# Convolution and scan of a three-block kernel: memory steps behind the weight items, two sums ahead of a tile's taps, chunk loads ahead of small vectors

## The chip, the cores and the metric

The kernel runs as one program on one core of a Trainium2 chip. The metric is the device time of an execution in microseconds; runs of the kernel before took 3612.26, 3619.60 and 3623.09 us (median 3619.6). One execution more was profiled: it took 3616.24 us. PE is TensorE, DVE VectorE, ACT ScalarE, POOL GpSimd; SP only issues transfers.

## The reference, cut to what matters

Three transformer-like blocks follow one another over 1024 positions of width 1024. The change lies in the first, with one piece of work of the second beside it:

```
proj = h @ w_in                                   # h (1024, 1024)
z, xbc, dt_f, dt_b, q, k, v, g = split(proj)
xbc = silu(centred_dwconv(xbc, conv_w, conv_b))   # 5 taps in time, by channel
xs, Bm, Cm = split(xbc)                           # 1024 + 256 + 256 channels
y = bidirectional_ssd(xs, softplus(dt + bias), A, Bm, Cm, D)   # chunks of 128 positions
lam = exp(sum(lq1*lk1)) - exp(sum(lq2*lk2)) + lam_init
```

Inside `bidirectional_ssd`, each direction sums `dt * A` over the time steps of a chunk (`a_cs`), takes exponentials of the sums and of their differences to the chunk's end, and carries a state from chunk to chunk. The second block attends to a memory of 256 rows; its keys and values, `mem_2 @ w_mem_kv_2`, depend on no activation and are computed beside the convolution of block one ("memory" below).

## The kernel before

Every engine has its own instruction list, written out by hand, and runs it in order; engines wait for each other through counting semaphores. There is no planner: the order in the functions is the order on the engine.

**Convolution (`sp_conv`, `pe_conv`, `act_conv`, `dve_conv`, `pool_conv`).** The projection comes in items of 128 channels. For an item SP loads a 512 KB weight slice, ACT makes its high part (`act_item`, L490), DVE its low part (`dve_item`, L497), and PE does 48 products of 128 x 512 (L508: three combinations of high and low, 8 slices of the inner dimension, 2 halves) into one of two PSUM pairs. Item 0 gives the time steps `dt`, items 1 to 12 the twelve channel tiles of `xbc`, items from 13 on queries and keys, which PE works off in quarters during the scan. In round r PE transposes the finished tile of two rounds before (the "turn"; tiles 10 and 11, at r = 4 and 5, have none) and does item r + 1. ACT in round r copies the turned tile out (L606, L610), applies silu to the tile before (L617), copies item r + 1 out of PSUM (`raw`, L622, which raises `conv_raw`), and makes the high part of item r + 3. DVE in round r waits for that copy (L683), does the five taps (L693 to L697), the low part of item r + 3, and then a piece of the time steps' chain (r = 2 to 5), memory's low part (r = 6, `dve_memory`, L1927), the sums (r = 8, L709 to L712) or `dt_end` (r = 9).

**Memory.** `pe_memory` has three steps, at r = 4, 5 and 6, ahead of the round's item: 8 transposes, 8 transposes, 64 products of 128 x 256 (L184) into banks 6 and 7. ACT copies each step's result as the last thing of the round (`act_memory`, L1918, L1920, L1921); step 1 waits for step 0's copy, step 2 for step 1's. The turn at r = 7 uses the same banks and waits for both of the last step's results:

```
if n == 3:
    pe.wait_ge(S["mem_out"], 3)
    pe.wait_ge(S["mem_lo"], 1)
```

**Sums.** At r = 8, behind item 9, PE forms the sums of `dtA` (6 small products, banks 6 and 7, `cum_mm`). DVE copies them to `cum` and subtracts (`cum_sub`); ACT exponentiates (`carry`, L636, first). The turn at r = 9 uses bank 7 again and waits for `carry` (`steps` at 1, in the list of PE).

**Scan.** `conv_over` makes each engine wait until the last turned tile has been stored to DRAM. Then SP issues, in this order: the gate vector `gssm` and four lambda vectors (each broadcast to 128 partitions), the first chunk of `xs` (512 KB), the spills of two query halves (`qk_out`, two transfers each), the second chunk. POOL scales the first chunk (L1041), PE makes the first state from it (L897, after three quarters of queries and keys), DVE copies the state. Eight rounds go backward in time, eight forward. `lambda_dots` (L1087 to L1093) comes first in DVE's list for the scan; its result is read by ACT after the backward rounds (L1001), `gssm` by DVE in the forward rounds (L1175). SP's transfers go through `Transfers.start` (L124): there are 8 semaphores in turn, and each issue waits until the transfer eight places before it has landed.

Of the kernel before, what the change touches and what calls it, by code (L numbers as in the profile page):

```python
# [8 lines left out]
S = 1024  # L9
# [154 lines left out]
def rows(vector, n=P):  # L164
    return vector.partition_broadcast(n)
# [371 lines left out]
def pe_conv(K):  # L537
    pe, S, m = K.pe, K.S, K.p2

    def item(n):  # L540
        pe.wait_ge(S["it_lo"], n + 1)
        for q in range(4):
            last = item_quarter(K, n, K.pair[n % 2], q)
        last.then_inc(S["it_mm"], 1)

    pe.wait_ge(S["nat_act"], NAT_N)
    item(0)
    for r in range(14):
        turn = r - 2
        if r == 13:  # L550
            pe_quarters(K, QK_FIRST)
        if turn >= 0 and CONV_TILES[turn] < 10:
            done = K.BT[:, CONV_TILES[turn] - 8] if CONV_TILES[turn] >= 8 else m.acc[turn % 3]
            n = turn if turn < 2 else turn - 2
            if n == 1:
                pe.wait_ge(S["dt_v"], 1)
            elif n == 5:
                pe.wait_ge(S["steps"], 1)
            if n >= 2:
                pe.wait_ge(S["conv_out"], n - 1)  # L560
            if n == 3:
                pe.wait_ge(S["mem_out"], 3)
                pe.wait_ge(S["mem_lo"], 1)
            pe.wait_ge(S["conv_silu"], turn + 1)
            transposed(pe, K.pair[2 + n % 2], [done[:, s * P:(s + 1) * P] for s in range(ST)], K.eye).then_inc(S["conv_turned"], 1)
        if 4 <= r < 7:
            pe_memory(K, r - 4)
        if r < 12:
            if r >= 1:
                pe.wait_ge(S["conv_raw"], r - 1) if r >= 2 else pe.wait_ge(S["dt_copied"], 1)  # L570
            item(r + 1)
        if r == 1:
            for st in range(ST):
                last = pe.transpose(K.bank[6][:, st * 32:(st + 1) * 32], m.dtT[0:32, st * P:(st + 1) * P], K.eye[0:32, 0:32])
            last.then_inc(S["dt_turned"], 1)
        if r == 8:
            pe.wait_ge(S["dtA"], 1)
            pe.wait_ge(*K.loads["upper"])
            pe.wait_ge(*K.loads["lower"])
            pe.wait_ge(S["conv_out"], 4)  # L580
            products(pe, K.bank[6][:, 0:128], [(K.upper, K.dtA[:, :, 0:16])])
            products(pe, K.bank[6][:, 128:256], [(K.lower, K.dtA[:, :, 16:32])])
            products(pe, K.bank[7][:, 0:256], [(K.ones, K.dtA)]).then_inc(S["cum_mm"], 1)
# [57 lines left out]
def dve_conv(K):  # L641
    v, S, vs, m = K.v, K.S, K.vs, K.p2

    def then(instruction):
        vs.mark(instruction)
        v.wait_ge(vs.sem, vs.n)

    v.wait_ge(S["nat_mm"], 5 * ST)
    for n in range(2):
        dve_item(K, n)  # L650
    norm_over(K, v)
    for raw in m.raw:
        vs.mark(v.memset(raw[:, 0:2], 0.0))
        vs.mark(v.memset(raw[:, 2 + S_LEN:], 0.0))
    v.wait_ge(vs.sem, vs.n)
    V, u, z, z2, dt = K.spare, K.dtA, K.cum, K.to_end, K.dt
    dve_item(K, 2)

    def time_steps():
        v.wait_ge(S["dt_u"], 1)  # L660
        then(v.tensor_scalar(z, u, 2.0, None, ALU.add))
        then(v.reciprocal(z, z))
        then(v.tensor_tensor(z, z, u, ALU.mult))
        then(v.tensor_tensor(z2, z, z, ALU.mult))
        then(v.tensor_scalar(dt, z2, 1.0 / 19, 1.0 / 17, ALU.mult, ALU.add))
        for n in range(15, 0, -2):
            then(v.tensor_tensor(dt, dt, z2, ALU.mult))
            then(v.tensor_scalar(dt, dt, 1.0 / n, None, ALU.add))
            if n in (13, 7, 3):
                yield  # L670
        then(v.tensor_tensor(dt, dt, z, ALU.mult))
        then(v.tensor_scalar(V, V, 0.0, None, ALU.max))
        then(v.scalar_tensor_tensor(dt, dt, 2.0, V, ALU.mult, ALU.add))
        v.wait_ge(S["A_exp"], 1)
        then(v.tensor_scalar(K.A32, K.A32, -1.0, None, ALU.mult))
        v.tensor_tensor(K.dtA, dt, over(K.A32, 1, ST), ALU.mult).then_inc(S["dtA"], 1)
        yield

    steps = time_steps()
    v.wait_ge(*K.loads["conv_w"])  # L680
    for r in range(12):
        tile = CONV_TILES[r]
        v.wait_ge(S["conv_raw"], r + 1)  # L683
        if r >= 3:
            old = CONV_TILES[r - 3]
            if old < 10:
                v.wait_ge(S["conv_turned"], (r - 3 if r - 3 < 2 else r - 5) + 1)
            v.wait_ge(S["conv_silu"], r - 2)
        raw, acc = m.raw[r % 2], m.acc[r % 3]
        for j in range(TAPS):  # L690
            tap = K.convw[:, tile, j:j + 1]
            if j == 0:
                then(v.tensor_scalar(acc, raw[:, 0:S_LEN], tap, None, ALU.mult))  # L693
            elif j < TAPS - 1:
                then(v.scalar_tensor_tensor(acc, raw[:, j:j + S_LEN], tap, acc, ALU.mult, ALU.add))
            else:
                v.scalar_tensor_tensor(acc, raw[:, j:j + S_LEN], tap, acc, ALU.mult, ALU.add).then_inc(S["conv_tap"], 1)  # L697
        dve_item(K, r + 3)
        if r == 1:
            v.wait_ge(S["dt_turned"], 1)  # L700
            v.wait_ge(*K.loads["dt_bias0"])
            v.wait_ge(*K.loads["dt_bias1"])
            v.tensor_tensor(V, K.bank[6][:, 0:256].rearrange("p (s n) -> p s n", s=ST), over(K.bias32, 1, ST), ALU.add).then_inc(S["dt_v"], 1)
        if 2 <= r < 6:
            next(steps)
        if r == 6:
            dve_memory(K)
        if r == 8:
            v.wait_ge(S["cum_mm"], 1)  # L709
            sums = K.bank[6][:, 0:256].rearrange("p (d s h) -> p s d h", d=2, s=ST)  # L710
            then(v.tensor_copy(K.cum.rearrange("p s (d h) -> p s d h", d=2), sums))
            v.tensor_tensor(K.to_end, K.bank[7][:, 0:256].rearrange("p (s n) -> p s n", s=ST), K.cum, ALU.subtract).then_inc(S["cum_sub"], 1)  # L712
        if r == 9:
            v.wait_ge(S["steps"], 2)
            v.tensor_tensor(K.dt_end, dt, K.to_end, ALU.mult).then_inc(S["dt_end"], 1)
    dve_quarters(K, QK_FIRST)
# [97 lines left out]
def sp_scan(K):  # L814

    sp, S, L, m = K.sp, K.S, K.loads, K.p3
    conv_over(K, sp)
    L.start(sp, "gssm", m.gssm, rows(K.dr["ssm_norm_g"][0]))
    for i, n in enumerate(("lambda_q1", "lambda_k1", "lambda_q2", "lambda_k2")):
        L.start(sp, n, K.p4.lq[:, i], rows(K.dr[n][0]))  # L820

    def chunk(r):
        if 2 <= r < ST + 2:
            sp.wait_ge(S["sc_xfree"], r - 1)
        elif r >= ST + 2:
            sp.wait_ge(S["sc_y"], 2 * (r - 2 - ST) + 2)
        if r < 2 * ST:
            L.start(sp, ("xs", r), m.xs[r % 2], K.xs_dram[CHUNKS[r]])

    def gate(c):  # L830
        if c:
            sp.wait_ge(S["sc_ms"], c)
        L.start(sp, ("zg", c), m.zg, K.nat_dram["z"][c])

    def back(c):

        if c >= ST:
            return
        if c >= 2:
            sp.wait_ge(S["sc_yadd"], 2 * (c - 1) + 1)  # L840
        for done in (0, 1):
            sp.wait_ge(*K.stores[("yb", done)])
        L.start(sp, ("yb", c), m.yb if c else m.y[0], K.yb_dram[c])

    def parts(x):

        cols = slice(x % 2 * 512, (x % 2 + 1) * 512)
        sp.wait_ge(S["qk_lo"], x + 1)
        for part in range(2):
            L.start(sp, ("qk_out", x, part), K.qk_dram[x // 2, part][:, cols], m.qk[x % 3][part].bitcast(F32))  # L850

    def quarters(ks):
        for k in ks:
            if k % 4 == 0 and k:
                sp_item(K, QK_ITEM + k // 4 + 2)
            if k % 2:
                parts(k // 2)

    chunk(0)
    quarters(QK_FIRST)  # L860
    chunk(1)
    for r in range(2 * ST):
        if r == ST:
            back(0)
        if r >= ST:
            gate(r - ST)
            back(r - ST + 1)
        for place in QK_PLAN[r]:
            quarters(place)
        chunk(r + 2)  # L870
# [233 lines left out]
def dve_scan(K):  # L1104
# [72 lines left out]
                vs.mark(last)  # L1177
        last.then_inc(S["sc_yn"], 1)

    lambda_dots(K)  # L1180
    v.wait_ge(*K.loads["eye"])
    vs.mark(v.tensor_tensor(K.below, K.lower, K.eye, ALU.subtract))
    vs.mark(v.tensor_tensor(K.above, K.upper, K.eye, ALU.subtract))
# [3 lines left out]
    for b in range(ST):  # L1187
# [12 lines left out]
        if b < ST - 1:  # L1200
            new_state(("bnew", b), b == 0)
        dve_quarters(K, QK_PLAN[b][2])
    lambda_sum(K)
    masked(0)
    both(0, 0)
# [2514 lines left out]
```

## Time and profile before

| | |
|---|---|
| three runs | 3612.26, 3619.60, 3623.09 us |
| profiled execution: time, span | 3616.24 us, 3614.4 us |
| PE busy in the span | 3141.3 us (87%) |
| DVE, ACT, POOL busy | 2060.6 (57%), 1197.4 (33%), 436.6 (12%) us |
| mean granted clock of PE | 0.94 |
| convolution (item 0 to last chunk stored) | about 316 to 534 us |
| backward half, forward half of the scan | about 534 to 676, to 915 us |

Times inside the profile count from the first instruction. A group's name is "output <- inputs" by the program's tile names; `banks` is PSUM. The bracket at the end of a timeline row is how long the engine was idle before the instruction and what ended it. Matmuls overlap, so their single durations add up to more than the time they take: the distance from start to start is the time. The granted clock is a share of the full 2.4 GHz.

### The profile page before, as it was taken

The numbers are of one execution on the slowest core, as the hardware profiler recorded it, in microseconds if no ns is written. First come the engines' busy times: TensorE is split into PE (matmuls) and PEld (weight loads), VectorE is DVE, ScalarE is ACT, GpSimd is POOL, SyncE is SP. The second block draws the span as 40 slices with busy tenths as digits, with TensorE's granted clock in tenths as the row PEclk, the third lists the DMA queues.
The fourth block names the chain that finished last, engine by engine and source line by source line (L and its number), as shares of the span: only waits on it lengthen the run. The fifth ranks groups of instructions, "written<-read, shape, count | busy, mean of one in ns | idle before, by whom it ended". The sixth has DMA issues, their size and how long they took to land. (4 is left out here: it accounts for less than half of the span.)

```text
span 3614.4 us, 37560 instructions
## 1 busy us (share of the span) xinstructions
PE 3141.3 (87%) x14208; PEld 2393.5 (66%) x14208; DVE 2060.6 (57%) x3113; ACT 1197.4 (33%) x2280; POOL 436.6 (12%) x407
## 2 busy tenths in 40 slices
PE   6999889886788879899997762989976989999999
PEld 5787667664677768677885552444554468888887
DVE  5112544487688835839886876549865334444444
ACT  2211231586566632234225651000264011112111
POOL 2000002344011100222340031010000000000000
PEclk9999999997899999999998986999988999999999
DMA  6323125433633334341462410411011011111111
GB/s 215 134 72 101 42 83 189 140 119 103 165 94 94 88 143 149 99 101 53 129 201 85 129 59 31 161 69 56 14 35 62 0 47 47 47 47 47 47 58 59
DMA packets 189934, 326.63 MB, mean 90 GB/s; under 512 B 16242, under 2 KB 110610, under 8 KB 189754
## 3 DMA queue, kind: packets, MB, share of 16 engines
q1 hardware_dynamic: 168602, 250.29, 22.7%
q0 software_dynamic: 21152, 73.94, 5.7%
q8 instruction: 114, 1.87, 0.2%
q14 instruction: 66, 0.54, 0.1%
HBM read 233.71 MB, written 89.16 MB: 89 GB/s over the span
## 5 line engine op out<-in xcount | busy, mean ns | idle before, releaser
L215 PE MATMUL banks<-b3h4a_hi,b3mlpw_part 128*128 128x512 f32 x1024 | 319.8, 391 | 6.8 <-DVE b3mlpw_part L3277 6.8
L215 PE MATMUL banks<-b3mlpw_part,b3mlp_acthi 128*128 128x512 f32 x1024 | 315.2, 389 | 0.0
L215 PE MATMUL banks<-b1ln_w,b_hThi 128*128 128x512 f32 x768 | 239.5, 393 | 0.0
L215 PEld LDWEIGHTS banks<-b3h4a_hi,b3mlpw_part 128*128 128x128 f32 x1024 | 193.7, 189 | 47.5 <-issue 7.1
L215 PEld LDWEIGHTS banks<-b3mlpw_part,b3mlp_acthi 128*128 128x128 f32 x1024 | 192.2, 188 | 39.9
L3324 DVE TENSOR_TENSOR b3out_x<-b3out_x,banks 128x1024 f32<-128x1024 f32 x128 | 154.8, 1219 | 111.6 <-PE banks L215 111.6
L215 PE MATMUL banks<-b3out_lo,b3mlpw_part 128*128 128x512 f32 x512 | 200.4, 391 | 0.0
L215 PE MATMUL banks<-b3mlpw_part,b3mlp_actlo 128*128 128x512 f32 x512 | 199.2, 389 | 0.0
L508 PE MATMUL banks<-b_hThi,b1item_hi 128*128 128x512 f32 x464 | 196.2, 423 | 3.4 <-DVE b1item_lo L497 3.1
L3294 ACT ACTIVATE b3mlp_relu<-banks 128x1024 f32<-128x1024 f32 x32 | 32.9, 1029 | 499.5 <-PE banks L215 499.5
L508 PE MATMUL banks<-b_hThi,b1item_lo 128*128 128x512 f32 x464 | 183.4, 395 | 0.0
L508 PE MATMUL banks<-b_hTlo,b1item_hi 128*128 128x512 f32 x464 | 183.4, 395 | 0.0
L2131 PE MATMUL banks<-b2h_hi,b2h_whi 128*128 128x512 f32 (+1 forms) x448 | 177.9, 397 | 5.9 <-issue 5.9
L1370 ACT ACTIVATE b1att_map<-b1att_map,fixed_stat 128x1024 f32<-128x1024 f32 x128 | 147.0, 1149 | 104.5 <-DVE fixed_stat L1419 104.1
L2320 DVE MAX8 b2late_top<-b2late_sel 128x8 f32<-128x384 f32 (+5 forms) x192 | 170.9, 890 | 16.8 <-DMA dv_spill<-b2ring_row 13.1
L3313 DVE TENSOR_TENSOR b3mlp_relu<-b3mlp_relu 128x1024 f32<-128x1024 f32 x32 | 39.2, 1225 | 243.5 <-ACT b3mlp_relu L3294 243.5
L2131 PE MATMUL banks<-b2h_lo,b2h_whi 128*128 128x512 f32 (+1 forms) x448 | 176.6, 394 | 0.0
L2131 PE MATMUL banks<-b2h_hi,b2h_wlo 128*128 128x512 f32 (+1 forms) x448 | 176.3, 393 | 0.0
L2322 DVE MATCH_REPLACE8 b2late_sel<-b2late_top,b2late_sel 128x384 f32<-128x384 f32 (+5 forms) x192 | 168.2, 876 | 0.0
L215 PEld LDWEIGHTS banks<-b1ln_w,b_hThi 128*128 128x128 f32 x768 | 144.6, 190 | 32.8 <-ACT b1ln_out L377 1.7
L1419 DVE CUSTOM_DVE_ANT_0 b1att_map<-banks,b1att_dist 128x1024 f32<-128x1024 f32 x128 | 151.6, 1222 | 0.6
L215 PE MATMUL banks<-b1ln_w,b_hTlo 128*128 128x512 f32 x384 | 150.3, 391 | 0.0
(417 smaller groups left out, 6716.8 us busy)
## 6 DMA issues: line engine op xcount, KB each, us to landing
qk_spill<-b1scan_qk SPq DMA_DIRECT2D x64, 256.0 KB, 2.8
b1att_k<-qk_spill SPq DMA_DIRECT2D x64, 256.0 KB, 8.2
b1out_ws<-in_w_out SPq DMA_DIRECT2D x16, 1024.0 KB, 5.0
b3mlpw_stage<-in_w_mlp_up SPq DMA_DIRECT2D x16, 1024.0 KB, 5.3
b3mlpw_stage<-in_w_mlp_down SPq DMA_DIRECT2D x16, 1024.0 KB, 4.9
b2h_stage<-in_w_in SPq DMA_DIRECT2D x30, 512.0 KB, 4.1
b1item_stage<-in_w_in SPq DMA_DIRECT2D x29, 512.0 KB, 4.9
b1ln_stage<-in_w_in SPq DMA_DIRECT2D x12, 1024.0 KB, 6.8
```

The costliest lines, as they stand in the source:

```text
L215: last = pe.matmul(out, x, y, start=i == 0, stop=i == n - 1)
L508: last = K.pe.matmul(pair[:, ss], a, b, start=q % 2 == 0 and i == 0, stop=q % 2 == 1 and i == 11)
L1370: a.activation(mp, mp, ACT.Exp, bias=s[:, i:i + 1], scale=-1.0, accum_out=s[:, 2 + i:3 + i]).then_inc(S["att_exp"], 1)
L1419: v.tensor_tensor_reduce(mp, K.pair[1 + i], m.dist[:, x0:x0 + S_LEN], -1.0, 3e38, ALU.add, ALU.min, s[:, i:i + 1]).then_inc(S["att_shift"], 1)
L2131: last = pe.matmul(K.bank[x % 2][0:w], a[:, k, 0:w], b[:, k, ss], start=part == 0 and i == 0, stop=part == 1 and i == 11)
L2320: vs.mark(v.max(top, view))
L2322: vs.mark(v.match_replace(view, top, view, TAKEN))
L3294: a.activation(m.tmp[i % 3], pair, ACT.Relu).then_inc(S["ml_relu"], 1)
L3313: v.tensor_tensor(tmp, tmp, tmp, ALU.mult).then_inc(S["ml_sq"], 1)
L3324: v.tensor_tensor(K.m4.x3[:, st], K.m4.x3[:, st], pair, ALU.add).then_inc(S["ml_acc"], 1)
```

## The change

Three edits of order, with no arithmetic added or left out. On PE, at r = 4, 5, 6, the memory step stands behind the round's item. On DVE, at r = 8, the copy of the sums and the subtraction stand ahead of the wait for the round's raw tile. In the scan SP issues the first two chunks first, then the lambda vectors, the first spills, and then the gate vector; DVE does the lambda dot products behind the first backward round.

```diff
@@ pe_conv @@
-        if 4 <= r < 7:
-            pe_memory(K, r - 4)
         if r < 12:
             if r >= 1:
                 pe.wait_ge(S["conv_raw"], r - 1) if r >= 2 else pe.wait_ge(S["dt_copied"], 1)
             item(r + 1)
+        if 4 <= r < 7:
+            pe_memory(K, r - 4)
@@ dve_conv @@
     for r in range(12):
         tile = CONV_TILES[r]
+        if r == 8:
+            v.wait_ge(S["cum_mm"], 1)
+            sums = K.bank[6][:, 0:256].rearrange("p (d s h) -> p s d h", d=2, s=ST)
+            then(v.tensor_copy(K.cum.rearrange("p s (d h) -> p s d h", d=2), sums))
+            v.tensor_tensor(K.to_end, K.bank[7][:, 0:256].rearrange("p (s n) -> p s n", s=ST), K.cum, ALU.subtract).then_inc(S["cum_sub"], 1)
         v.wait_ge(S["conv_raw"], r + 1)
...
         if r == 6:
             dve_memory(K)
-        if r == 8:
-            v.wait_ge(S["cum_mm"], 1)
-            sums = K.bank[6][:, 0:256].rearrange("p (d s h) -> p s d h", d=2, s=ST)
-            then(v.tensor_copy(K.cum.rearrange("p s (d h) -> p s d h", d=2), sums))
-            v.tensor_tensor(K.to_end, K.bank[7][:, 0:256].rearrange("p (s n) -> p s n", s=ST), K.cum, ALU.subtract).then_inc(S["cum_sub"], 1)
@@ sp_scan @@
     conv_over(K, sp)
-    L.start(sp, "gssm", m.gssm, rows(K.dr["ssm_norm_g"][0]))
-    for i, n in enumerate(("lambda_q1", "lambda_k1", "lambda_q2", "lambda_k2")):
-        L.start(sp, n, K.p4.lq[:, i], rows(K.dr[n][0]))
...
     chunk(0)
+    chunk(1)
+    for i, n in enumerate(("lambda_q1", "lambda_k1", "lambda_q2", "lambda_k2")):
+        L.start(sp, n, K.p4.lq[:, i], rows(K.dr[n][0]))
     quarters(QK_FIRST)
-    chunk(1)
+    L.start(sp, "gssm", m.gssm, rows(K.dr["ssm_norm_g"][0]))
@@ dve_scan @@
-    lambda_dots(K)
     v.wait_ge(*K.loads["eye"])
...
         dve_quarters(K, QK_PLAN[b][2])
+        if b == 0:
+            lambda_dots(K)
```

## Rows read from the trace of the kernel before

**Rows 1.** The page, busy time by engine: us, share of the span, instructions.
```profile
PE 3141.3 (87%) x14208; PEld 2393.5 (66%) x14208; DVE 2060.6 (57%) x3113; ACT 1197.4 (33%) x2280; POOL 436.6 (12%) x407
```

**Rows 2.** Waits of PE, 374 to 476.2 us: total us, times, longest.
```profile
PE banks L206 <- DVE b1conv_mk L1927: 9.1, 1, 9.1
PE banks L206 <- ACT b1ssm_carry L636: 8.7, 1, 8.7
PE banks L206 <- ACT b1conv_memT L1918: 3.0, 1, 3.0
PE banks L184 <- ACT b1conv_memT L1918: 2.2, 1, 2.2
```

**Rows 3.** Timeline of PE: start us, us, engine, line, operation, [idle before <- releaser].
```profile
404.36 5.38 PE L184 MATMUL banks<-b1conv_memT,b1conv_wkv 128*128 128x256 f32 x16 [2.19 <-ACT b1conv_memT L1918]
...
409.57 3.62 PE L184 MATMUL banks<-b1conv_wkv,b1conv_memT 128*128 128x256 f32 x16
...
440.15 1.94 PE L206 MATMUL banks<-fixed_eye,b1conv_acc 128*128 128x128 f32 x8 [9.12 <-DVE b1conv_mk L1927]
...
454.47 1.03 PE L206 MATMUL banks<-fixed_eye,b1conv_acc 128*128 128x128 f32 x8
...
466.69 0.60 PE L184 MATMUL banks<-b1ssm_dtA,fixed_ones 128*128 128x256 f32 x2
...
475.94 1.97 PE L206 MATMUL banks<-fixed_eye,b1conv_acc 128*128 128x128 f32 x8 [8.65 <-ACT b1ssm_carry L636]
...
489.48 1.04 PE L206 MATMUL banks<-fixed_eye,b1conv_acc 128*128 128x128 f32 x8
...
501.25 1.04 PE L206 MATMUL banks<-fixed_eye,b1conv_acc 128*128 128x128 f32 x8
```

**Rows 4.** Busy time in four stretches; after POOL the granted clock, DMA share, GB/s.
```profile
386.30:389.30 3.00, 0.03 (x2) 0.02 (x1) 1.80 (x2) 2.88 (x3) 0.00 (x0) 1.00 0.00 0
454.50:466.30 11.80, 11.80 (x58) 9.90 (x57) 7.03 (x6) 4.05 (x4) 0.89 (x1) 1.00 0.31 90
467.30:476.00 8.70, 0.06 (x1) 0.06 (x1) 7.79 (x8) 2.90 (x5) 0.00 (x0) 0.61 0.03 3
555.00:675.00 120.00, 119.07 (x479) 89.30 (x477) 55.65 (x53) 19.08 (x27) 26.58 (x18) 1.00 0.55 180
```

**Rows 5.** Timeline of ScalarE, round 6 and round 8.
```profile
432.93 0.59 ACT L1920 ACTIVATE b1conv_mk<-banks 128x512 fp32r<-128x512 f32 x1
...
468.44 1.28 ACT L636 ACT_TABLE_LOAD   x1
475.51 0.38 ACT L636 ACTIVATE b1ssm_carry<-banks 128x256 f32<-128x256 f32 x1 [5.79 <-DVE b1ssm_to_end L712]
```

**Rows 6.** Timeline of VectorE, round 6 and round 8.
```profile
439.21 0.68 DVE L1927 TENSOR_TENSOR b1conv_mk<-banks,b1conv_mk 128x512 fp32r<-128x512 f32 x1
...
467.51 0.75 DVE L693 TENSOR_SCALAR b1conv_acc<-b1conv_raw,b1ssm_convw 128x1024 f32<-128x1024 f32 x1 [4.61 <-ACT b1conv_raw L622]
...
474.60 0.42 DVE L711 COPY b1ssm_cum<-banks 128x256 f32<-128x256 f32 x1
475.05 0.42 DVE L712 TENSOR_TENSOR b1ssm_to_end<-banks,b1ssm_cum 128x256 f32<-128x256 f32 x1
```

**Rows 7.** Timeline of all engines at the scan's front (SPq: transfers issued by SP).
```profile
533.93 0.34 SPq L128 DMA_DIRECT2D b1scan_gssm<-in_ssm_norm_g  x1
...
536.22 0.43 SPq L128 DMA_DIRECT2D b1scan_xs<-x_spill  x1
...
541.84 0.23 DVE L1093 CUSTOM_DVE_ANT_0 b1ssm_spare<-b1ssm_spare 128x64 f32<-128x64 f32 x1 [13.42 <-DMA b1ssm_spare<-in_lambda_k]
...
543.04 1.90 POOL L1041 TENSOR_TENSOR b1scan_scaled<-b1scan_xs,b1ssm_dt_end 128x1024 f32<-128x1024 f32 x1 [12.37 <-DMA b1scan_xs<-x_spill]
...
545.08 1.19 PE L897 MATMUL banks<-b1scan_scaled,b1ssm_B 128*128 128x512 f32 x1 [10.45 <-POOL b1scan_scaled L1041]
```

**Rows 8.** The chunk tile `xs` of the scan: its 16 loads, issue to landing.
```profile
DMA to landing us min/median/max: 3.7/5.2/5.7
```

## The prediction

> **What bounds the kernel now.** I read the page first: one core, and of its span of 3614.4 us TensorE (PE) is busy 87% [rows 1]. The share says little about a change that touches only some 300 us of the first block, so I went to the waits of PE in the stretch from the first memory transposes to the second half of the convolution. In these 102 us PE stands still four times, 23.0 us in all: twice for ScalarE's copy of the transposed memory (2.97 and 2.19 us), once for VectorE's low part of the memory keys (9.12), once for ScalarE's exponential `carry` (8.65) [rows 2]. The timeline of PE then shows what a wait costs beyond itself. A regular tile (8 transposes and a weight item of 48 products) takes 489.48 to 501.25 = 11.77 us; the tile after the 9.12 us wait takes 440.15 to 454.47 = 14.32, the one after the 8.65 us wait 475.94 to 489.48 = 13.54, and the first 16 memory products 5.38 us where the next 16 take 3.62 [rows 3]. Over the 8.65 us wait the granted clock averages 0.61, so it went from 2.4 to 1.2 GHz in it; over the wait of 2.97 us it stayed at 1.00 [rows 4]. Outside these waits PE is dense here: in the undisturbed tile from 454.5 to 466.3 us PE is busy 11.80 of 11.80, VectorE, with its taps and an item's low part, 7.03 [rows 4]. So in this stretch each microsecond that PE no longer waits should end the stretch earlier by one, and its lateness is handed on: from 555 to 675 us PE is busy 119.07 of 120 at clock 1.00 [rows 4], and the stages after that start from what PE has finished.
>
> **Part 1: memory's steps behind the items.** PE is in order. At r = 4, 5, 6 it now does item r + 1 first and then the memory step. Nothing the item needs is later than before: its low part was made two rounds earlier, its PSUM pair was emptied a round and a half earlier. The copy of the first transposes by ScalarE now has an item of 11 us beside it, as has that of the second. Both waits (2.97 + 2.19 = 5.2 us) go. Split the 11.77 us of a tile into 0.8 for transposes and 11.0 for the item, and count from the start of round 4: item 5 ends at 11.0, memory 0 at 11.8, item 6 at 22.8, memory 1 at 23.6, the turn at 24.4, item 7 at 35.4. The 64 memory products follow: their four groups of 16 take 3.5 us each (the next group starts a little before the 3.62 are over; the first took 5.38 for the slow clock, 1.76 more), so until 49.3. What is late next is the turn at r = 7, which still needs both memory results. Before, the high copy by ScalarE came at 432.93 although the products had long ended, as it sat behind the copy of item 7's result, and VectorE's subtraction at 439.21, behind five taps and an item [rows 5, 6]. Now item 7 ends 13.9 us ahead of the products: ScalarE has copied it about 1 us later, VectorE has done taps and low part 7 us after that, at 43.6, and both stand ready 5.7 us early. The new wait is 0.59 + 0.68 and two hand-overs, 1.5 us. Queued behind it on PE is item 8, and ScalarE's round 7. The 9.12 becomes 1.5, and at 1.5 us I expect the clock to hold, as it did over 2.97: of 14.32 us the tile gives back 14.32 - 11.77 = 2.55.
> Sum of part 1: 2.97 + 2.19 + 9.12 + 1.76 + 2.55 - 1.5 = 17.1 us. If the clock falls all the same it is 14.5, the lower end; 18.6 (no wait left) is the upper.
>
> **Part 2: the sums ahead of the taps at r = 8.** VectorE's copy and subtraction (0.42 each, at 474.60 and 475.05) move ahead of the wait for the tile's raw copy. PE's last sum ends at 466.69 + 0.60 = 467.29 [rows 3]; VectorE is idle then (4.61 us until its taps at 467.51 [rows 6]), so both are done by about 468.25. ScalarE has its raw copy and item copy first, then a table load from 468.44 to 469.72, which before stood ahead of its wait [rows 5]; the exponential of 0.38 now follows at once and ends at 470.1. PE's turn starts at 470.15 in place of 475.94: 5.8 us. The table load is what is late next. The price is that this tile's taps start at about 468.3 in place of 467.51, 0.8 us; PE needs their result only a full tile (11.77 us) later, against 7.0 us of work: nothing. VectorE parked ahead of the taps would cost something only if the sums came after the raw copy by more than that slack; before, they came within 0.2 us of it.
> The clock: PE then rests 467.29 to 470.15, 2.9 us. The rows show both answers for about this length: 1.00 throughout in one rest of 2.97 us [rows 4], and slow products at 404.36 after a rest of 2.19 behind light transposes [rows 3]. The sums are short too, so I leave the lost 13.54 - 11.77 = 1.8 us where it is. Part 2 gives 5.8, with ends at 5.0 (the taps' delay passed on once) and 7.6.
>
> **Part 3: the scan's front.** SP issued the gate vector at 533.93, four lambda rows, and the first chunk at 536.22; GpSimd began on it at 543.04, 12.37 us idle, and PE on the first state at 545.08 [rows 7]. Now the chunk is issued first: 2.3 us by the issue times alone, if it then takes as long as before. Before, it needed 543.04 - 536.22 = 6.8 us to be used, the longest way among the chunk loads, which land in 3.7 to 5.7 us, median 5.2 [rows 8]; ahead of it were 512 KB of the vector and the lambda rows, the last of which reached VectorE only at 541.84 [rows 7]. Issued first at 533.93 it is usable at 533.93 + 3.8 = 537.7 at best and 539.7 at worst, a gain of 5.3 to 3.4. The second chunk directly behind it carries another 512 KB, and so I take a way of 4.6 us, between the shortest and the median, which is a gain of 4.5. The low end is 2.3, the high end 5.3.
> The Trainium skill (DMA: Bandwidth & Descriptors, Queues, rings and completion order) says that each DMA engine takes descriptors in the order of its ring. By that the second chunk can't hold up the first, and part 3 would be 5.3 and the whole sum 28.2; the rows don't show two chunks back to back.
> VectorE's wait for the lambda rows (13.42 us, until 541.84) goes from the front; it held back nothing that PE waited for, and the dot products (0.23 us and a little more, twice) now lie beside a busy PE. ScalarE wants them only behind the backward half, and the gate vector is read in the forward half. On SP the lambda issues and the four spills now stand ahead of the vector; each issue waits for the one eight places earlier, so the next item load goes out about when it did, and PE asks for it five quarters of an item later, at 11.0 / 4 = 2.8 us each: nothing. If it were late by the longest landing of a load of its size here, 5.7 us [rows 8], so much would be lost again.
>
> **The sum.** 17.1 + 5.8 + 4.5 = 27.4 us. The profiled execution took 3616.24 us, 1.8 more than its span: 3588.8 from its own time. It lies 3.4 under the median of the three runs, 3619.6, and 2.1 under their mean, 3618.3. I take the mean as the base: 3590.9, told as 3591. The parts' ends give 14.5 + 5.0 + 2.3 = 21.8 to 18.6 + 7.6 + 5.3 = 31.5 us.
>
> **Rivals.**
> *A, the forecast*, 3591, 82%.
> *B, the memory's subtraction stays late.* If VectorE were still in its taps when the high copy comes, the wait at r = 7 would be about 9 us again and with it the slow clock: 27.4 - 7.6 - 2.55 = 17.2, so 3601. For it: exactly this order made the 9.12. Against: taps begin with item 7's copy, and copy, taps and low part are 8.2 us against 13.9 of memory products. 6%.
> *C, the gain is handed on only in part.* A load or a later stage takes over (the item load behind the lambda rows, the chunk loads, the attention's front) and gives back half: 3605. Against: item loads are issued two rounds ahead, 23 us against landings of 5.7, and PE is 99% busy behind. 5%.
> *D, it does nothing that shows*: the stretch is bound by another engine, 3615 to 3620. Against: VectorE and ScalarE themselves wait on PE here. 4%.
> *E, slower: the clock pays it back.* Without these rests PE runs dense from 374 to 675. If it were then held at 1.2 GHz, each microsecond of work would take two: from 27 us of such work on it decides, and 40 us of the backward scan held down would end at 3631. For it: nothing in the rows but that the clock is granted and taken. Against: 120 us at 99% busy kept 1.00 [rows 4]. 3%. The Trainium skill (TensorE: Matmul & The Clock Gate, Part 1) knows such a limit only once three cores of a die run dense matmuls; here one does.
>
> **The numbers.** A measurement of this kernel tells about 0.3%, 11 us, from no change: 3629 and 3607 are the bounds around the mean. A, B and nearly all of C are faster: 0.92; D and the rest of C the same: 0.05; E slower: 0.03. The range reaches from A's upper end with the spread of the runs, 3583, to beyond B, 3603.
>
> **What would show it.** PE's waits for `memT` gone; the turn at r = 7 waiting 1.5 us for `mk`, the one at r = 9 about 2.9 for `carry`; the 64 memory products in 13.9 us; the last convolution tile 23 us earlier, GpSimd's first scaled chunk 3.8 to 5.8 us after SP's first issue, PE's wait for it 6 in place of 10.45 us. Wrong if the wait for `mk` stays above 5 us, if tiles between grow beyond 11.8, if GpSimd's first operation comes later than 6 us after the issue, or if the 27 us are there at 550 and gone at 900.

## The result, and the profile after

The changed kernel takes 3592.02 us (median of 6 runs, 3587.31 to 3594.58) against 3621.24 us for the kernel before on the same chip (6 runs, 3612.26 to 3624.18): ratio 0.9921, 95% interval 0.9908 to 0.9934, so 0.8% or 29 us faster. Run a second time beside 21 runs of the kernel before (median 3618.35) it took 3592.25, ratio 0.9932 (0.9919 to 0.9944), 26 us. The forecast was 3591, with 27.4 us gained. The profiled execution took 3593.28 us, its span is 3591.5, 22.9 us under that of before.

The page after, span and busy time (as [rows 1]):

```profile
span 3591.5 us, 37561 instructions
...
PE 3146.4 (88%) x14208; PEld 2400.0 (67%) x14208; DVE 2061.1 (57%) x3113; ACT 1198.3 (33%) x2280; POOL 435.1 (12%) x407
```

The waits of TensorE (PE) from 374 to 460 us, as in [rows 2] (total us, times, longest). Of the four waits the two for `memT` are gone, and 9.1 and 8.7 us have become 1.6 and 2.9:

```profile
PE banks L206 <- ACT b1ssm_carry L636: 2.9, 1, 2.9
PE banks L206 <- DVE b1conv_mk L1928: 1.6, 1, 1.6
```

PE's timeline, as in [rows 3]. All four groups of memory products take 3.62 us now. The tile behind the wait for the keys takes 423.91 to 435.74 = 11.83 us, a regular one; the tile behind the wait for `carry` 451.43 to 464.91 = 13.48 (before 13.54):

```profile
408.32 3.62 PE L184 MATMUL banks<-b1conv_memT,b1conv_wkv 128*128 128x256 f32 x16
411.77 3.62 PE L184 MATMUL banks<-b1conv_wkv,b1conv_memT 128*128 128x256 f32 x16
...
423.91 1.06 PE L206 MATMUL banks<-fixed_eye,b1conv_acc 128*128 128x128 f32 x8 [1.61 <-DVE b1conv_mk L1928]
...
435.74 1.04 PE L206 MATMUL banks<-fixed_eye,b1conv_acc 128*128 128x128 f32 x8
...
447.95 0.60 PE L184 MATMUL banks<-b1ssm_dtA,fixed_ones 128*128 128x256 f32 x2
451.43 1.73 PE L206 MATMUL banks<-fixed_eye,b1conv_acc 128*128 128x128 f32 x8 [2.88 <-ACT b1ssm_carry L636]
...
464.91 1.04 PE L206 MATMUL banks<-fixed_eye,b1conv_acc 128*128 128x128 f32 x8
```

What released the two waits, ScalarE (ACT) first, VectorE (DVE) second; they answer to [rows 5, 6]. The low part of the keys now comes right behind the high part; the sums come ahead of the taps; the exponential comes right behind its table load:

```profile
422.33 0.60 ACT L1921 ACTIVATE b1conv_mk<-banks 128x512 fp32r<-128x512 f32 x1 [11.84 <-PE banks L184]
...
449.70 1.28 ACT L636 ACT_TABLE_LOAD   x1
450.99 0.38 ACT L636 ACTIVATE b1ssm_carry<-banks 128x256 f32<-128x256 f32 x1
```

```profile
422.97 0.69 DVE L1928 TENSOR_TENSOR b1conv_mk<-banks,b1conv_mk 128x512 fp32r<-128x512 f32 x1 [6.21 <-ACT b1conv_mk L1921]
...
448.59 0.42 DVE L686 COPY b1ssm_cum<-banks 128x256 f32<-128x256 f32 x1 [4.41 <-PE banks L184]
449.05 0.42 DVE L687 TENSOR_TENSOR b1ssm_to_end<-banks,b1ssm_cum 128x256 f32<-128x256 f32 x1
449.39 0.74 DVE L698 TENSOR_SCALAR b1conv_acc<-b1conv_raw,b1ssm_convw 128x1024 f32<-128x1024 f32 x1
```

Busy time in four stretches, as in [rows 4] (behind POOL the granted clock): the rest ahead of the keys, the tile behind it, the rest ahead of `carry`, and what followed it. The clock stays at 1.00 in both rests, holds after the first and falls to 1.2 GHz after the second:

```profile
421.80:424.00 2.20, 0.59 (x4) 0.21 (x3) 0.69 (x1) 1.09 (x2) 0.00 (x0) 1.00 0.00 0
424.00:436.00 12.00, 12.00 (x59) 10.04 (x60) 0.00 (x0) 2.12 (x3) 0.89 (x1) 1.00 0.15 45
448.50:451.40 2.90, 0.05 (x1) 0.00 (x0) 2.74 (x4) 2.87 (x5) 0.00 (x0) 1.00 0.00 0
451.40:455.00 3.60, 3.57 (x13) 3.18 (x14) 3.49 (x4) 2.37 (x4) 0.49 (x1) 0.54 0.02 5
```

The scan's front, as in [rows 7], and the landings of the chunk loads, as in [rows 8]. GpSimd begins 513.02 - 509.37 = 3.65 us after the first issue, in the kernel before 543.04 - 533.93 = 9.11; PE waits 5.01 in place of 10.45 us. The pair shown here is the widest one: over the profiles of this study this way takes 8.46 to 9.11 us in the three kernels with the old order of SP and 3.65 to 4.04 us in the eight profiles with the new one, so part 3 is worth 4.4 to 5.5 us there. The rows:

```profile
509.37 0.81 SPq L128 DMA_DIRECT2D b1scan_xs<-x_spill  x2
...
510.23 0.42 SPq L128 DMA_DIRECT2D b1ssm_spare<-in_lambda_q  x1
...
513.02 1.90 POOL L1041 TENSOR_TENSOR b1scan_scaled<-b1scan_xs,b1ssm_dt_end 128x1024 f32<-128x1024 f32 x1 [6.91 <-DMA b1scan_xs<-x_spill]
514.69 0.33 SPq L128 DMA_DIRECT2D b1scan_gssm<-in_ssm_norm_g  x1
...
515.06 3.75 PE L897 MATMUL banks<-b1scan_scaled,b1ssm_B 128*128 128x512 f32 x4 [5.01 <-POOL b1scan_scaled L1041]
...
525.17 0.22 DVE L1093 CUSTOM_DVE_ANT_0 b1ssm_spare<-b1ssm_spare 128x64 f32<-128x64 f32 x1
```

```profile
DMA to landing us min/median/max: 3.5/4.4/6.4
```

The start times of the same work in both profiles show where the time came from and where some of it went again:

| starts at, us | before | after | earlier by |
|---|---|---|---|
| first item's products | 315.6 | 314.3 | 1.3 |
| last of the sums | 466.7 | 448.0 | 18.7 |
| turn at r = 9 | 475.9 | 451.4 | 24.5 |
| first state | 545.1 | 515.1 | 30.0 |
| first, last product of `R` in the forward half | 681.4, 884.4 | 650.9, 857.0 | 30.5, 27.4 |
| first attention scores | 909.4 | 882.1 | 27.3 |
| last relu of the third block's MLP | 3566.4 | 3543.5 | 22.9 |

The 1.3 us at the top lie ahead of any change. From there to the turn at r = 9 the gain is 23.2 us, from there to the first state another 5.5, 28.7 in all.

### The profile page after: what moved, and what is told of

It reads as the page before. It is cut to its first block and busy times, and to the rows that moved or that the text cites. A ratio compares the mean times of both kernels' runs of the same rounds, so it can differ in the third digit from the quotient of the medians.

```text
span 3591.5 us, 37561 instructions
## 1 busy us (share of the span) xinstructions
PE 3146.4 (88%) x14208; PEld 2400.0 (67%) x14208; DVE 2061.1 (57%) x3113; ACT 1198.3 (33%) x2280; POOL 435.1 (12%) x407
```

## The experiments

**Each part alone, and the whole once more.** Three kernels hold one of the three edits each, as the diff of the change shows it; the fourth is the changed kernel unaltered. All four are compared with the same 21 runs of the kernel before.

> Part 1 alone (memory's steps behind the items), all else as before. My theory: 17.1 us shorter than the kernel before, the wait for memT gone, the wait for the memory keys 1.5 us, the wait for carry still 8.7 and the wait for the first scaled chunk still 10.5. Rival (the three parts are not additive, the wait for carry only shows since others were removed or grows): under 12 us. Rival (the subtraction stays behind the taps): 10 us, with a wait of about 9 for the keys.

Measured: 3603.59 us against 3618.35, ratio 0.9961 (0.9949 to 0.9974), 14.8 us by the medians, 9 to 18 by the interval. In its trace the sums start at 448.0 and the first item at 314.3, to the tenth as in the changed kernel, so the stretch gained the same 17.4 us. PE's waits there, with those for `carry` and for the chunk still in place:

```profile
PE banks L897 <- POOL b1scan_scaled L1041: 9.8, 1, 9.8
PE banks L206 <- ACT b1ssm_carry L636: 8.7, 1, 8.7
PE banks L206 <- DVE b1conv_mk L1927: 1.6, 1, 1.6
```

> Part 2 alone (the sums ahead of the taps at r = 8). My theory: 5.8 us shorter; the wait for carry 2.9 in place of 8.65 us, the tile behind it still slow (13 to 13.5 us). If the clock holds over 2.9 us: 7.6. Rival (the later taps are handed on to PE): 5.0 or less, and the next turns come late. Rival (nothing, the stretch is bound elsewhere): 0.

Measured: 3613.11 against 3618.35, ratio 0.9986 (0.9977 to 0.9995), 5.2 us. The wait for `carry` is 2.9 us, the four others as before. From the sums to the first state it gained 7.2 - 0.4 = 6.8 us by start times, of which 0.7 belong to a shorter wait for the chunk (9.8 against 10.5).

> Part 3 alone (first two chunks, then lambda, spills, gate vector; lambda dots behind the first backward round). My theory: 4.5 us shorter, up to 5.5, with PE's wait for the first scaled chunk 5 to 6 in place of 10.45 us. Rival (the later order of SP's transfers costs the forward half or the attention's front what the front gains, which would explain that in the changed kernel 30.5 us at the first forward chunk are 27.3 at the first attention scores): 0 to 2 us shorter in total, and the forward half some 3 us longer than in the kernel before.

Measured: 3614.52 against 3618.35, ratio 0.9993 (0.9984 to 1.0002). The 3.8 us by the medians are not clear of nothing in the times alone; the trace has PE's wait at 5.1 in place of 10.45 us and the first state 7.2 - 1.9 = 5.3 us earlier than the sums. Its forward half took 673.7 to 880.0 = 206.3 us, 3.3 more than in the kernel before, as the rival has it. But the kernels with part 1 and part 2 alone, whose scan is that of the kernel before, took 208.0 and 207.8 us there, so this is no cost of part 3.

> The changed kernel once more, nothing altered. Theory (what is lost behind the front, 30.5 us at the first forward chunk to 22.9 at the end of the span, is mostly chance of single executions, the clock's turns above all): the forward half of the scan takes 204 to 207 us in this profile, not the same as in the first one, and the ratio is again 0.992. Rival (a cost of the change itself): again 207 us for the forward half and the same losses behind it.

Measured: 3592.25 us, ratio 0.9932 (0.9919 to 0.9944). The forward half took 208.1 us (652.0 to 860.1) where the first profile of the same kernel took 206.1: its length is not fixed by the code. Over the fourteen profiles of this study it took 202.9 to 203.0 us in six (the kernel before and five altered ones), 206.0 to 206.3 in four, and 207.8 to 208.1 in four. The 3 us that the pair of profiles loses there go with no edit; that they are the chance of single executions fits the repeated kernel, and fits that the profiled execution of before (3616.24) is faster than its kernel's medians (3617 to 3621), but with one profile of before it is not shown. The stretch behind it, from the last product of `R` to the last relu of the third block, varies as well: 2682.0 us before, 2686.5 in the first profile of the changed kernel, 2684.0 in the repeated one; of the fourteen profiles the kernel before has the shortest. So of the 4.5 us that the pair loses there, 2.5 go with no edit. The three parts' gains, 14.8 + 5.2 + 3.8 = 23.8 us, stand beside 26.1 for the whole against the same runs; the difference is within the intervals.

**Memory's last step alone put back.** In the changed kernel the 64 products stand ahead of item 7 again:

```diff
+        if r == 6:
+            pe_memory(K, 2)
         if r < 12:
...
-        if 4 <= r < 7:
+        if 4 <= r < 6:
             pe_memory(K, r - 4)
```

> The changed kernel with one thing undone: at r = 6 the 64 memory products stand ahead of item 7 again, while the two transposing steps stay behind their items. My theory (VectorE's subtraction gets behind the taps by this order alone, and a wait this long brings the slow clock): PE's wait for the keys 9.1 in place of 1.6 us, the tile behind it 14.3 in place of 11.8, so 10 us slower than the changed kernel and 16 us faster than the kernel before. Rival (the waits for memT, 5.2 us, carried most of part 1): 5 us slower than the changed kernel or less.

Measured: 3601.97 us, ratio 0.9952 (0.9940 to 0.9964); 9.7 us slower than the changed kernel's 3592.25, or 7 to 11 us by the ratios (0.9932 and 0.9921), as the two were measured on different chips. PE's timeline has the wait and the slow tile back, 430.72 to 444.66 = 13.94 us:

```profile
396.60 3.69 PE L184 MATMUL banks<-b1conv_memT,b1conv_wkv 128*128 128x256 f32 x16 [1.32 <-ACT b1conv_memT L1921]
...
430.72 1.94 PE L206 MATMUL banks<-fixed_eye,b1conv_acc 128*128 128x128 f32 x8 [9.15 <-DVE b1conv_mk L1930]
...
444.66 1.04 PE L206 MATMUL banks<-fixed_eye,b1conv_acc 128*128 128x128 f32 x8
```

From the turn at r = 2 to the last of the sums the trace has 456.87 - 347.07 = 109.8 us where the changed kernel has 447.95 - 349.35 = 98.6: 11.2 us longer (counted from there, as item 0 ran partly at the low clock in the changed kernel's profile, 0.72 over 314 to 320 us, and not in this one), of which 1.32 are a wait for `memT` that this order brings back. So the order of this one step is worth more than half of the 17.4 us of part 1, and the rest is in the main the two short waits for `memT` and the slow products behind the second. The rival, 5 us or less, is out by the trace.

**What held the first chunk back.** Three orders of SP at the scan's front, one profile each, all else as changed: the gate vector first; the four lambda vectors first; the second chunk behind the spills.

```diff
 # gate vector first
+    L.start(sp, "gssm", m.gssm, rows(K.dr["ssm_norm_g"][0]))
     chunk(0)
...
 # lambda vectors first
+    for i, n in enumerate(("lambda_q1", "lambda_k1", "lambda_q2", "lambda_k2")):
+        L.start(sp, n, K.p4.lq[:, i], rows(K.dr[n][0]))
     chunk(0)
...
 # second chunk late
     chunk(0)
-    chunk(1)
...
     quarters(QK_FIRST)
+    chunk(1)
```

> The changed kernel with the gate vector (512 KB broadcast) issued ahead of the first chunk. Theory 1 (bytes ahead in the queue hold the chunk back): GpSimd begins 5 to 6 us after SP's first issue where the changed kernel has 3.65 us, and PE waits 6.5 to 7 in place of 5.0. Theory 2 (the four small lambda broadcasts did it): GpSimd begins 4.1 us after the first issue, 0.4 later by the issue alone, PE waits 5.4.

> The changed kernel with the four lambda vectors (32 KB each, in pieces of 256 bytes) issued ahead of the first chunk. Theory 1 (bytes count): GpSimd begins 5.7 us after SP's first issue, 1.9 us for the four issues and 0.1 for 128 KB more. Theory 2 (the small pieces are slow, few bytes moved from 537 to 539 us in the kernel before): 7 us or more after the first issue, and PE waits 8.3 us or more.

> The changed kernel with the second chunk's load behind the first spills again. By the prediction's choice (the second chunk behind the first holds it up by some 0.9 us) GpSimd would begin 2.8 us after SP's first issue in place of 3.65; by the ring rule there is no difference, 3.65, as the first chunk is served first.

First issue and GpSimd's start in the timelines, gate vector first, then lambda first, then with the second chunk late:

```profile
509.79 0.34 SPq L128 DMA_DIRECT2D b1scan_gssm<-in_ssm_norm_g  x1
...
510.18 0.90 SPq L128 DMA_DIRECT2D b1scan_xs<-x_spill  x2
...
515.72 1.90 POOL L1041 TENSOR_TENSOR b1scan_scaled<-b1scan_xs,b1ssm_dt_end 128x1024 f32<-128x1024 f32 x1 [9.17 <-DMA b1scan_xs<-x_spill]
```

```profile
509.59 0.34 SPq L128 DMA_DIRECT2D b1ssm_spare<-in_lambda_q  x1
...
511.40 0.90 SPq L128 DMA_DIRECT2D b1scan_xs<-x_spill  x2
...
518.19 1.90 POOL L1041 TENSOR_TENSOR b1scan_scaled<-b1scan_xs,b1ssm_dt_end 128x1024 f32<-128x1024 f32 x1 [11.85 <-DMA b1scan_xs<-x_spill]
```

```profile
509.27 0.34 SPq L128 DMA_DIRECT2D b1scan_xs<-x_spill  x1
...
512.78 1.90 POOL L1041 TENSOR_TENSOR b1scan_scaled<-b1scan_xs,b1ssm_dt_end 128x1024 f32<-128x1024 f32 x1 [6.76 <-DMA b1ssm_spare<-in_lambda_k]
```

In the last of these rows the profile names a lambda row as what ended the wait; GpSimd's list waits there for the chunk alone. From first issue to GpSimd it is 5.93 us, 8.60 us and 3.51 us, against 3.65 in the first profile of the changed kernel and 3.65 to 4.04 in all eight with its order of SP. The 512 KB of the gate vector cost 1.9 to 2.3 us, of which 0.4 are the issue; the four lambda vectors with a quarter of the bytes cost 4.6 to 4.95, of which 1.8 are issues. Theory 1 held for the vector (though PE waited 7.3 us, not 6.5 to 7), theory 2 for the lambda rows: they are slow out of proportion to their bytes. With the lambda rows first, few bytes move until they are through, as two stretches behind the last of their issues show (the last figure is GB/s):

```profile
512.60:514.60 2.00, 0.00 (x0) 0.00 (x0) 0.00 (x0) 0.00 (x0) 0.00 (x0) 0.54 0.05 13
514.60:516.60 2.00, 0.00 (x0) 0.00 (x0) 0.00 (x0) 0.00 (x0) 0.00 (x0) 0.50 0.71 269
```

Whether it is the 256-byte pieces or the number of transfers was not tried. The second chunk behind the first costs 0.14 us against the first profile and 0.5 at most against the eight, not the 0.9 that the prediction allowed for. PE waits 7.3, 9.9 and 4.8 us in the three. Their single times, 3589.95, 3592.80 and 3590.20 us, are too few to tell 2 to 5 us.

**Work for the wait that is left.** The changed kernel, with one entry of the plan of quarters altered:

```diff
-        for n in (1, 2, 2) if r < ST else ...
+        for n in (1, 4, 0) if r == 0 else (1, 2, 2) if r < ST else ...
```

> The changed kernel with all four remaining quarters of the first backward round ahead of the first state (plan 1, 4, 0 in place of 1, 2, 2). Theory (PE only waits for the first scaled chunk as its list has nothing else ahead of it, and the slow clock behind the wait costs again): the wait of 5.0 us and the slow clock go, 6 to 8 us faster than the changed kernel. Rival (the state is needed at once, so it only moves the wait to the next step): 0 to 2 us.

Measured: 3592.91 us, ratio 0.9937 (0.9924 to 0.9949): nothing gained. The wait for the chunk is 0.80 us and the four products behind it run at full clock (1.96 us, where the changed kernel's take 3.75), but a new wait of 6.33 us stands at the next step:

```profile
515.34 1.96 PE L897 MATMUL banks<-b1scan_scaled,b1ssm_B 128*128 128x512 f32 x4 [0.80 <-POOL b1scan_scaled L1041]
...
526.39 3.78 PE L886 MATMUL banks<-b1scan_state,b1ssm_CT 128*128 128x512 f32 x4 [6.33 <-DVE b1scan_state L1128]
```

The lists of ACT and DVE in the same stretch say why. DVE's copy of the state (L1128) now stands behind the low part of the next item (L497), that behind ACT's high part (L490), and that behind the item's load, which SP issued at 515.37, behind chunks, lambda rows, spills and gate vector, and which took 7.5 us to land:

```profile
514.82 0.46 SPq L128 DMA_DIRECT2D b1scan_gssm<-in_ssm_norm_g  x1
...
515.37 0.39 SPq L128 DMA_DIRECT2D b1item_stage<-in_w_in  x1
...
522.89 1.06 ACT L490 ACTIVATE b1item_hi<-b1item_stage 128x1024 fp32r<-128x1024 f32 x1 [5.77 <-DMA b1item_stage<-in_w_in]
...
523.98 1.23 DVE L497 TENSOR_TENSOR b1item_lo<-b1item_stage,b1item_hi 128x1024 fp32r<-128x1024 f32 x1 [6.12 <-ACT b1item_hi L490]
525.12 1.22 DVE L1128 COPY b1scan_state<-banks 128x1024 f32<-128x1024 f32 x1
```

**The table load earlier.** The three exponentials of r = 8 ahead of `act_item(K, r + 3)`, and both edits together:

```diff
             a.activation(m.raw[r % 2]..., ACT.Copy).then_inc(S["conv_raw"], 1)
+            if r == 8:
+                a.wait_ge(S["cum_sub"], 1)
...
             act_item(K, r + 3)
...
-        if r == 8:
-            a.wait_ge(S["cum_sub"], 1)
```

> The changed kernel with ScalarE's three exponentials at r = 8 ahead of the item's high part. Theory (the table load is what is late next, and it can start 1.05 us earlier): PE rests 1.8 to 1.9 in place of 2.9 us ahead of the turn at r = 9; 1.0 us faster if the clock falls all the same, 2.8 if it holds, which the tile behind shows (13.5 us fallen, 11.8 held). Rival (the clock is not moved by 1 us of rest and other steps hide it): 0.

Measured: 3587.17 us, ratio 0.9919 (0.9906 to 0.9933); the kernel with the dots first, whose time is not told apart from that of the changed kernel, has 0.9927 against the same runs. The rest is 1.93 in place of 2.88 us, 1.0 us gained. The clock fell all the same, a little later; its tile takes 449.75 to 463.22 = 13.47 us:

```profile
449.75 1.09 PE L206 MATMUL banks<-fixed_eye,b1conv_acc 128*128 128x128 f32 x8 [1.93 <-ACT b1ssm_carry L625]
...
463.22 1.04 PE L206 MATMUL banks<-fixed_eye,b1conv_acc 128*128 128x128 f32 x8
```

```profile
447.80:449.70 1.90, 0.02 (x1) 0.00 (x0) 1.77 (x4) 1.87 (x4) 0.00 (x0) 1.00 0.00 0
449.70:451.00 1.30, 1.25 (x10) 1.15 (x11) 1.26 (x2) 1.30 (x3) 0.00 (x0) 0.94 0.07 13
451.00:454.00 3.00, 3.00 (x9) 2.32 (x8) 2.93 (x3) 2.46 (x3) 0.89 (x1) 0.50 0.01 5
```

The other 2 to 4 us of its median are not explained by this; its profile is one of the six with the short forward half. Its interval overlaps those of the changed kernel (0.9921 and 0.9932): it is the fastest version run, and what the trace shows of it is 1 us.

> Both of these edits on the changed kernel. Theory (they are independent): their gains add up, 7 to 11 us faster than the changed kernel, some 0.990 of the kernel before less 0.2 points or more. Rival: no more than the larger of the two.

Measured: 3592.21 us, ratio 0.9932 (0.9920 to 0.9944). The two gains don't add; PE's waits of 6.9 us for the state and 1.9 for `carry` are both in its trace. The theory failed with that of the run before.

**The lambda dots.** VectorE's list as before, SP's order as changed:

> The changed kernel with the lambda dot products first in VectorE's list for the scan again (SP's order as changed). Theory (VectorE's wait for the lambda rows held back nothing PE waited for): same time as the changed kernel within 1 us, PE's wait for the first scaled chunk 5.0 us as there. Rival (the masks, dtA_lo and the first low half behind the dots are what the front waits for): 2 us slower or more, with a new wait of PE on VectorE behind the first state.

Measured: 3590.23 us, ratio 0.9927 (0.9914 to 0.9941), PE's wait 5.4 us. DVE waits 12.34 us for the rows and copies the state at 519.17, 515.38 + 3.79, as in the changed kernel (518.85, 515.06 + 3.79). So moving the dots gives nothing that shows; part 3 is SP's order.

## Why the prediction was right

*The number.* The 3592.02 us lie 1 us from the forecast partly by luck. The kernel before had a median of 3621.24 us beside it, 2.9 us above the mean of three runs that the prediction took as its base, and the gain was 29.2 us, 1.8 above the sum. The sum itself holds: against the other 21 runs of the kernel before the gain is 26.1 us, and the two intervals reach from 20 to 33 us around the 27.4.

*The bound.* PE's lateness was handed on as foretold: 28.7 us gained between the first item and the first state, and 26 to 29 us by the runs.

*Part 1*, 17.1 us forecast: 17.4 in the trace. The rounds went as counted; the wait for the keys is 1.61 us (forecast 1.5), the products run at full clock, the tile behind takes 11.83. Term by term the waits gave 12.7 us, the first 16 products 1.76 and the tile 2.49, so 16.9 of the 17.4. Alone it measured 14.8, with 17.1 inside its interval.

*Part 2*, 5.8 forecast with the slow tile left in: wait 2.88 us (2.9), carry at 450.99 directly behind the table load, tile 13.48 (13.54). From the sums' end to the turn that is 5.77 us gained; alone it measured 5.2. Leaving the clock's loss in was right: even 1.93 us of rest did not save it. But it was a choice between two rows that said opposite things, and what decides it stays open, so that part of the term is a lucky choice and not an understood one.

*Part 3*, 4.5 forecast: 5.46 us from first issue to GpSimd in the pair of profiles (9.11 to 3.65), 4.4 to 5.5 over all of them. The pair lies 0.2 above the part's upper end of 5.3, and GpSimd's start at 3.65 us just ahead of the 3.8 to 5.8 that the prediction gave as its sign; PE's wait is 5.0 us where it said 6. What was too large is the 0.9 us for the second chunk, which costs 0.14 to 0.5. The Trainium skill (DMA: Bandwidth & Descriptors, Queues, rings and completion order) says that each DMA engine takes descriptors in the order of its ring; that, and the 5.3 us which the prediction drew from it, agree with these 0.14 to 0.5 us and with the gain in the traces. What the prediction got half right is the cause: it named the 512 KB ahead of the chunk first; the 128 KB of lambda rows cost twice as much.

*Edits costed at nothing.* The later taps at r = 8 (449.39 in place of the raw copy's end at about 448.7) moved no turn: the next two tiles take 11.78 us each, as in the kernel before. The dots cost and gain nothing that shows (run with the dots first). The item load is issued 5.75 us after SP's first issue where the kernel before had 7.65, and no wait of PE for it shows; the run with the quarters pulled ahead shows how near it is to mattering.

*Rivals.* B (keys behind the taps) is excluded by the 1.6 us, and its mechanism came back when one step was put back: 9.7 us. C (the gain handed on in part): the pair of profiles seems to say so, 30.5 us to 22.9, but the 3 us lost in the forward half go with no edit over fourteen profiles, and the medians keep 26 to 29 us. The 4.5 us lost behind it, over 2700 us, are not traced to a place; 2.5 of them go with no edit, and runs of one kernel spread by 7 to 12 us. So a small loss of the change's own behind the scan is not ruled out. D fell by the times. E fell by the clock: it is 1.00 from 525 to 645 us with PE busy 118.52 of 120, and its mean over the execution is 0.942 against 0.940.

## What to carry to other kernels

On an in-order engine, put the step whose input has just been asked for behind a step whose input is already there; what it gains is the wait, the time at the low clock behind it, and often a second wait, as the consumer's engine is then free when the result comes. Before filling a wait that is left, follow the lists of the engines that make the next input: work pulled ahead on one engine is pulled ahead in the others' lists too, with its loads. Judge a change of 0.8% by medians of several runs and use profiles for places and waits: two profiles of one kernel differ by 2 us in a stretch that has nothing to do with the change, and by up to 0.4 us in a single wait for a transfer.

## What the runs showed of the hardware that I had not expected

- The granted clock fell to 1.2 GHz after a rest of 1.93 us that came behind a dense tile and six small products, about 1.1 us after PE had begun again with transposes (an estimate from the clock of 0.94 over 449.7 to 451.0); it stayed at 1.00 over and after a rest of 1.61 us, and over one of 2.97 us in the kernel before [rows 4]. The length of the rest alone doesn't decide it. What does stays open.
- Four broadcasts of 256-byte rows, 32 KB each, issued ahead of a 512 KB load delayed its use by 4.6 to 4.95 us (1.8 of them issues), a broadcast of 512 KB ahead of it by 1.9 to 2.3, and a load of 512 KB issued behind it by 0.14 to 0.5.
- The forward half of the scan has three lengths, 203, 206 and 208 us, in profiles of kernels that are alike there. Which one comes was not settled.
